# Sums of squares ahead of the two MLPs: eight stored squares added by VectorE, channel sum after the second unit

## The chip, the cores and the metric

One core of a Trainium2 chip runs the whole program. The metric is the device time of one execution in microseconds (us), lower is better. TensorE (PE) multiplies matrices, VectorE (DVE), ScalarE (ACT) and GpSimd (POOL) work element by element, SyncE (SP) issues DMAs. Each engine takes its own instructions in order and waits for the others by semaphores.

## The reference

A two-layer decoder trunk on 512 tokens of width 1024, all in float32. Cut to what matters:

```python
def rmsnorm(x, g):
    y = x * lax.rsqrt(jnp.mean(x * x, axis=-1, keepdims=True) + EPS)
    return y * g

for i in range(2):
    h = h + mixer_i(rmsnorm(h, norm_mix[i]))          # 0: dilated windows, 1: differential
    h = h + squared_relu_mlp(rmsnorm(h, norm_mlp[i]), w_ff1[i], w_ff2[i])
    h = h + sigmoid(rmsnorm(h, norm_ple[i]) @ w_ple_gate[i]) * (p[i] @ w_ple_proj[i])
out = rmsnorm(h, final_norm)
# squared_relu_mlp: a = relu(h @ w1); return (a * a) @ w2,  1024 -> 4096 -> 1024
```

## The kernel before

The hidden state h is kept with channels on the 128 partitions: eight slabs (n = 0 to 7) of 128 channels by 512 tokens. Work on TensorE is cut into units. A unit makes 128 output channels: eight chunks of three matmuls of 128x512 (high times high, low times high, high times low), so 24 matmuls into one PSUM bank. For that each weight is split in two: ScalarE rounds the 128x1024 raw tile (`w_hi`, `split_hi`, L976), VectorE subtracts (`w_lo`, `split_lo`, L1284). Activations are split alike (`act_hi` L991, `act_lo` L1299). `next_hi(u)` and `next_lo(u)` split the weights of unit u+1. There are two sets of split weights, by the parity of the unit, so the split of unit u waits until unit u-2 is done: `wait(sc, units_done, u - 1)`.

Ahead of each MLP stands `out_late`. The attention's output projection has one (layer 0) or two (layer 1) late units that come slab by slab in PSUM, and the MLP's first unit is put between: for each slab VectorE adds the projection to h (L1529, L1532), ScalarE makes `act_hi` and the square (L1001, L1004), VectorE makes `act_lo` of the slab before, and TensorE does that slab's chunk of the first unit. So chunk n of the first unit waits for `act_lo` n.

The norm: the squares of the eight slabs are summed (the first one is written to `sumsq`, the other seven pass through two buffers `square`, and GpSimd adds each, L956). One matmul with ones sums over channels into bank `attn` (`statistics` on TensorE, L1828, two passes). ScalarE takes the root (L1009, which needs another activation table), VectorE the reciprocal `rstd` (L1304). `rstd` is applied only where a unit leaves PSUM: `scaled` = bank x `rstd` (L1552), `hidden` = max(scaled, 0) x scaled (L1555), `act_hi` (L1142), `act_lo` (L1558).

The banks set how late that may be. The MLP's first unit has `unit_out1`, the second `unit_out0`, the third `misc` (`is_third`), and the fourth `unit_out0` again. Thus the fourth unit of an MLP waits until the second has been read by L1552 (`wait(te, evac_done, ...)` in `unit`), and this comes after `rstd` and after the whole of the first unit's four steps in VectorE's order.

SyncE loads the raw weights ahead (`load`, L731), each once the split of the unit two before is done.

Of the kernel before, what the change touches and what calls it, by code (L numbers as in the profile page):

```python
# [33 lines left out]
F32 = mybir.dt.float32  # L34
F32R = mybir.dt.float32r
ALU = mybir.AluOpType
ACT = mybir.ActivationFunctionType

P = 128
T = 512  # L40
# [60 lines left out]


LATE = (1, 2)


U_A = 0
# [142 lines left out]
def build(nc, x, p, rel_bias, a_w_qkv, a_w_o, b_w_qkv, b_w_o, lq1, lk1, lq2, lk2, subln, norm_mix,  # L249
          norm_mlp, w_ff1, w_ff2, norm_ple, w_gate, w_proj, final_norm, selector, out):  # L250
    ctx = ExitStack()
    with ctx:
# [26 lines left out]
        heads = sb("heads", [P, 2 * GROUPS * 3 * T])  # L279
        bias = [sb(f"bias{i}", [P, 2 * T]) for i in range(2)]  # L280
        with nc.sbuf_tensor("soft", [P, 3, B_TILES * P], F32) as soft:
            pass
        probs = [sb(f"probs{i}", [P, 2 * T]) for i in range(A_ITEMS)]
        probs_t = sb("probs_t", [P, T])
# [309 lines left out]
        x_copied = sem("x_copied")  # L594
        square_ready = sem("square_ready")
        sumsq_done = sem("sumsq_done")
        act_hi_ready = sem("act_hi_ready")
        act_ready = sem("act_ready")
        ones_ready = sem("ones_ready")
# [271 lines left out]
        def _(pool):  # L871
# [78 lines left out]
                    spread_values(step)  # L950

            for norm in range(1, 7):
                for n in range(1, KC if norm < 6 else KC - 1):
                    pool.wait_ge(square_ready, (norm - 1) * (KC - 1) + n)
                    pool.wait_ge(sumsq_done, (norm - 1) * KC + n)
                    pool.tensor_tensor(sumsq[:, :], sumsq[:, :], square[n % 2][:, :],  # L956
                                       ALU.add).then_inc(sumsq_done, 1)
                for head in range(B_HEADS) if norm == 3 else ():
                    spread_head(head)
# [3 lines left out]
        def _(sc):  # L963
# [30 lines left out]
            def slab(w, n, h, dst, written, count):  # L994

                wait(sc, written, count)
                if dst is not None:
                    slab_hi(w, n, h, dst)
                if n == 0:
                    wait(sc, stat_ps, w // KC)  # L1000
                    sc.activation(sumsq[:, :], h[:, n, :], ACT.Square).then_inc(sumsq_done, 1)  # L1001
                else:
                    wait(sc, sumsq_done, w - 1 - KC)
                    sc.activation(square[w % 2][:, :], h[:, n, :], ACT.Square  # L1004
                                  ).then_inc(square_ready, 1)
# [114 lines left out]
            def out_late(layer, first, w0, h, dst):  # L1120

                late = LATE[layer]
                if layer:
                    for i in range(late):
                        next_hi(At(first + KC + i))
                for n in range(KC):
                    if n < KC - 1:
                        slab(w0 + n, n, h, dst, late_added, layer * (KC - 1) + n + 1)
                    else:
                        slab(w0 + n, n, h, dst, evac_done, first + KC + late)  # L1130

            def mlp_of(layer, first, norm, h):
                def up(u, k, n, is_first):
                    two_ahead = u.reg is None
                    if is_first or not two_ahead:
                        next_hi(u)
                    if two_ahead and n < KC - 1:
                        next_hi(u + 1)
                    if is_first:
                        statistics(norm)  # L1140
                    wait(sc, hid_ready, k + 1)
                    sc.activation(MID[layer][0][:, n, :], hidden[:, :], ACT.Copy  # L1142
                                  ).then_inc(hid_hi_ready, 1)
                    if layer == 0 and two_ahead and n == 1:
                        split_ple_hi(0)

                def down(u, q, n, last):
                    if last:
                        add_slab(u, (norm + 1) * KC + n, n, h, IN[layer])
                    else:  # L1150
                        next_hi(u)
                mlp(sc, layer, first, up, down)
# [124 lines left out]
        def _(ve):  # L1277
# [241 lines left out]
            def out_late(layer, first, w0, h, dst):  # L1519

                late = LATE[layer]
                u = first + KC + late - 1
                if layer:
                    for i in range(late):
                        next_lo(At(first + KC + i))
                for n in range(KC):
                    if n < KC - 1:
                        ve.wait_ge(late_ps, layer * (KC - 1) + n + 1)
                        ve.tensor_tensor(h[:, n, :], h[:, n, :], wide_bank(n), ALU.add).then_inc(late_added, 1)  # L1529
                    else:  # L1530
                        ve.wait_ge(units_done, u + 1)
                        ve.tensor_tensor(h[:, n, :], h[:, n, :], wide_bank(n), ALU.add).then_inc(evac_done, late)  # L1532
                    if n:
                        slab_lo(w0 + n - 1, n - 1, h, dst)
                    if layer == 0 and n == 5:
                        ve.wait_ge(units_done, first + KC)
                        ve.tensor_tensor(h[:, KC - 1, :], h[:, KC - 1, :], misc[:, :], ALU.add
                                         ).then_inc(evac_done, 1)
                        ve.wait_ge(evac_done, first + KC)
                slab_lo(w0 + KC - 1, KC - 1, h, dst)  # L1540

            def mlp_of(layer, first, norm, h):
                def up(u, k, n, is_first):
                    two_ahead = u.reg is None
                    if is_first or not two_ahead:
                        next_lo(u)
                    if two_ahead and n < KC - 1:
                        next_lo(u + 1)
                    if is_first:
                        statistics(norm)  # L1550
                    wait(ve, units_done, u + 1)
                    ve.tensor_tensor(scaled[:, :], bank_of(u)[:, :], rstd[:, :], ALU.mult  # L1552
                                     ).then_inc(evac_done, 1)
                    wait(ve, evac_done, u + 1)
                    ve.scalar_tensor_tensor(hidden[:, :], scaled[:, :], 0.0, scaled[:, :],  # L1555
                                            ALU.max, ALU.mult).then_inc(hid_ready, 1)
                    wait(ve, hid_hi_ready, k + 1)
                    ve.tensor_tensor(MID[layer][1][:, n, :], hidden[:, :], MID[layer][0][:, n, :],  # L1558
                                     ALU.subtract).then_inc(hid_done, 1)
                    if layer == 0 and two_ahead and n == 1:  # L1560
                        split_ple_lo(0)

                def down(u, q, n, last):
# [190 lines left out]
        def _(te):  # L1754
# [274 lines left out]

            def mlp_of(layer, first, norm):  # L2030
                def up(u, k, n, is_first):
                    if is_first:
                        statistics(norm)
                    else:
                        whole(u, IN[layer])
                    if layer == 0 and u.reg is None and n == 1:
                        turn_ple(0)
# [189 lines left out]
```

## Time and profile before

| | us |
|---|---|
| median of 3 runs | 1580.41 (1580.26 to 1580.99) |
| the profiled execution, whole | 1581.12 |
| its span, first to last record | 1579.3 |
| PE busy | 1557.7 (99%) |
| DVE busy | 930.8 (59%) |
| ACT busy | 585.7 (37%) |
| POOL busy | 502.3 (32%) |
| mean granted clock of TensorE | 0.996 |

The profiled execution is 1.82 us longer than its span, and 0.71 us longer than the median. A busy PE means that a matmul is in the pipeline; consecutive matmuls of 128x512 last 0.39 us each but start every 0.227 us. Times in the rows count from the span's start. Line numbers are those of the kernel before.

### The profile page before, as it was taken

The numbers are of one execution on the slowest core, as the hardware profiler recorded it, in microseconds if no ns is written. First come the engines' busy times: TensorE is split into PE (matmuls) and PEld (weight loads), VectorE is DVE, ScalarE is ACT, GpSimd is POOL, SyncE is SP. The second block draws the span as 40 slices with busy tenths as digits, with TensorE's granted clock in tenths as the row PEclk, the third lists the DMA queues.
The fourth block names the chain that finished last, engine by engine and source line by source line (L and its number), as shares of the span: only waits on it lengthen the run. The fifth ranks groups of instructions, "written<-read, shape, count | busy, mean of one in ns | idle before, by whom it ended". The sixth has DMA issues, their size and how long they took to land.

```text
span 1579.3 us, 22036 instructions
## 1 busy us (share of the span) xinstructions
PE 1557.7 (99%) x7890; PEld 1282.6 (81%) x7890; DVE 930.8 (59%) x1569; ACT 585.7 (37%) x1056; POOL 502.3 (32%) x900
## 2 busy tenths in 40 slices
PE   9999999999999999999999999999999999999998
PEld 7788888888888788888888878888778888888887
DVE  6466466567456854536355677778585453635565
ACT  5223324314324522212223445777452221312344
POOL 4067578488491200000001126888420000000111
PEclk9999999999999999999999999999999999999998
DMA  6565566465443233333333344454333333333331
GB/s 171 141 171 154 143 166 158 143 171 144 122 132 109 79 102 93 95 102 90 99 93 93 101 122 141 123 138 130 101 93 94 94 104 96 93 95 91 100 110 71
DMA packets 327204, 184.37 MB, mean 117 GB/s; under 512 B 44857, under 2 KB 312690, under 8 KB 327138
## 3 DMA queue, kind: packets, MB, share of 16 engines
q1 hardware_dynamic: 300112, 158.61, 35.3%
q0 software_dynamic: 26768, 24.88, 6.0%
q8 instruction: 38, 0.62, 0.2%
q14 instruction: 28, 0.23, 0.1%
q10 hardware_dynamic: 258, 0.04, 0.0%
HBM read 157.11 MB, written 10.60 MB: 106 GB/s over the span
## 4 chain that ended last, share of the span: by engine, by line
PE 81%; POOL 10%; DVE 2%; DMA 2%; SPq 2%; ACT 2%; issue 1%; POOLq 0%; ACTq 0%; DVEq 0%
PE unit_out L1757 22%; PE unit_out L1759 22%; PE unit_out L1758 22%; POOL probs L919 8%; POOL sumsq L956 1%; PE attn L2117 1%; PE unit_out L1922 1%; PE attn L1905 1%; SPq L763 1%; PE unit_out L1923 1%; PE unit_out L1924 1%; DMA w_raw<-in_a_w_qkv_dram 1%; DMA probs<-blocks 1%; DVE w_lo L1284 1%; PE misc L1757 1%
## 5 line engine op out<-in xcount | busy, mean ns | idle before, releaser
L1757 PE MATMUL unit_out<-act_hi,w_hi 128*128 128x512 f32 x1849 | 724.4, 392 | 2.4 <-DVE act_lo L1299 1.2
L1759 PE MATMUL unit_out<-act_hi,w_lo 128*128 128x512 f32 x1849 | 718.2, 388 | 0.0
L1758 PE MATMUL unit_out<-act_lo,w_hi 128*128 128x512 f32 x1849 | 718.0, 388 | 0.0
L976 ACT ACTIVATE w_hi<-w_raw 128x1024 fp32r<-128x1024 f32 (+3 forms) x256 | 271.2, 1059 | 505.8 <-PE unit_out L1759 412.3
L1757 PEld LDWEIGHTS unit_out<-act_hi,w_hi 128*128 128x128 f32 x1849 | 347.2, 188 | 78.6 <-DVE w_lo L1284 4.5
L1759 PEld LDWEIGHTS unit_out<-act_hi,w_lo 128*128 128x128 f32 x1849 | 347.2, 188 | 71.9
L1758 PEld LDWEIGHTS unit_out<-act_lo,w_hi 128*128 128x128 f32 x1849 | 347.4, 188 | 69.8 <-issue 0.2
L1284 DVE TENSOR_TENSOR w_lo<-w_raw,w_hi 128x1024 fp32r<-128x1024 f32 (+3 forms) x256 | 320.2, 1251 | 114.5 <-ACT w_hi L976 114.2
L956 POOL TENSOR_TENSOR sumsq<-sumsq,square 128x512 f32<-128x512 f32 x41 | 57.9, 1411 | 843.3 <-ACT square L1004 841.6
L919 POOL DMA_DIRECT2D probs<-blocks x448 | 221.3, 503 | 135.2 <-DVE blocks L1377 109.1
L928 POOL DMA_DIRECT2D heads<-probs_t x256 | 139.1, 552 | 67.4 <-DVE probs_t L1377 67.0
L1142 ACT ACTIVATE act_hi<-hidden 128x512 fp32r<-128x512 f32 x64 | 40.5, 633 | 243.4 <-DVE hidden L1555 243.4
L1552 DVE TENSOR_TENSOR scaled<-unit_out,rstd 128x512 f32<-128x512 f32 x62 | 42.8, 690 | 67.7 <-PE unit_out L1759 67.6
L1363 DVE TENSOR_TENSOR h_a<-h_a,unit_out 128x512 f32<-128x512 f32 x39 | 26.8, 688 | 90.0 <-PE unit_out L1759 90.0
L1363 DVE TENSOR_TENSOR heads<-heads,unit_out 128x512 f32<-128x512 f32 x40 | 27.5, 687 | 86.8 <-PE unit_out L1759 86.8
L928 POOL DMA_DIRECT2D soft<-soft_blocks x128 | 76.0, 602 | 7.4 <-issue 5.4
L1085 ACT ACTIVATE probs<-probs,w_raw 128x256 f32<-128x256 f32 (+1 forms) x128 | 61.7, 483 | 28.3 <-DVE w_raw L1393 28.3
L1558 DVE TENSOR_TENSOR act_lo<-hidden,act_hi 128x512 fp32r<-128x512 f32 x64 | 44.3, 693 | 44.7 <-ACT act_hi L1142 44.7
L1555 DVE SCALAR_TENSOR_TENSOR hidden<-scaled 128x512 f32<-128x512 f32 x64 | 44.3, 692 | 2.2
L1201 ACT ACTIVATE soft<-soft,low 128x512 f32<-128x512 f32 (+3 forms) x64 | 35.1, 551 | 7.2 <-DVE low L1639 7.1
L1468 DVE TENSOR_TENSOR act_lo<-attn,act_hi 128x512 f32 (+1 forms) x8 | 5.5, 692 | 53.0 <-ACT act_hi L1095 53.0
L1372 DVE TENSOR_SCALAR probs<-probs,w_raw 128x256 f32<-128x256 f32 (+1 forms) x128 | 35.5, 342 | 0.3
(316 smaller groups left out, 1399.8 us busy)
## 6 DMA issues: line engine op xcount, KB each, us to landing
w_raw<-in_w_ff_dram SPq DMA_DIRECT2D x128, 512.0 KB, 4.0
w_raw<-in_a_w_qkv_dram SPq DMA_DIRECT2D x56, 512.0 KB, 4.4
probs<-blocks POOLq DMA_DIRECT2D x448, 32.0 KB, 2.5
w_raw<-in_b_w_qkv_dram SPq DMA_DIRECT2D x24, 512.0 KB, 4.2
w_raw<-in_a_w_qkv_dram SPq DMA_DIRECT2D x32, 256.0 KB, 3.1
w_raw<-in_w_ple_gate_dram SPq DMA_DIRECT2D x16, 512.0 KB, 4.0
soft<-soft_blocks POOLq DMA_DIRECT2D x128, 40.0 KB, 1.9
heads<-probs_t POOLq DMA_DIRECT2D x256, 16.0 KB, 2.7
```

The source lines that it names most:

```text
L919: pool.dma_start(turned_order(to[j * SUB:(j + 1) * SUB, :])[:, i, :], turned_order(blocks_of[i * SUB:(i + 1) * SUB, :])[:, j, :]).then_inc ...
L928: pool.dma_start(to[j * SUB:(j + 1) * SUB, :, i, :], of[i * SUB:(i + 1) * SUB, j, :, :]).then_inc(landed, 16)
L956: pool.tensor_tensor(sumsq[:, :], sumsq[:, :], square[n % 2][:, :], ALU.add).then_inc(sumsq_done, 1)
L976: sc.activation(weights_of(u)[0][:, 0:width, :], w_raw[par][:, 0:width, :], ACT.Copy).then_inc(hi_done, 1)
L1085: e = sc.activation(probs[ph][:, cols], probs[ph][:, cols], ACT.Exp, bias=low_col, scale=-1.0, accum_out=sum_col)
L1284: ve.tensor_tensor(lo[:, 0:width, :], w_raw[par][:, 0:width, :], hi[:, 0:width, :], ALU.subtract).then_inc(lo_done, 1)
L1363: ve.tensor_tensor(h[:, n, :], h[:, n, :], unit_out[u.const % 2][:, :], ALU.add).then_inc(evac_done, 1)
L1555: ve.scalar_tensor_tensor(hidden[:, :], scaled[:, :], 0.0, scaled[:, :], ALU.max, ALU.mult).then_inc(hid_ready, 1)
L1558: ve.tensor_tensor(MID[layer][1][:, n, :], hidden[:, :], MID[layer][0][:, n, :], ALU.subtract).then_inc(hid_done, 1)
L1757: te.matmul(bank, w_k[0], hi, start=start, stop=False)
L1758: te.matmul(bank, w_k[0], lo, start=False, stop=False)
L1759: return te.matmul(bank, w_k[1], hi, start=False, stop=stop)
```

## The change

For the norms ahead of the two MLPs (numbers 1 and 4 in `TREE_NORMS`) three things are different. ScalarE writes the eight squares to eight places of a new tile `squares`, in memory that the attention's tiles had, without waiting for anyone. GpSimd adds nothing there. VectorE adds them in three instructions (`add_squares`: 2048, 1024 and 512 elements a partition) once all eight are there. TensorE's matmul with ones stands after the second unit instead of after the first. ScalarE loads the table of the root ahead, with a root of one column.

Besides, weights are split at other places. The second unit's are split inside `out_late`, on ScalarE before slab 6 and on VectorE before the add of slab 7 (before: after all slabs). The third's and the fourth's are split before the root and the reciprocal (before: the fourth's after the first unit's `act_lo`), and each later one a unit earlier in the code.

```diff
+TREE_NORMS = (1, 4)
...
+        with nc.sbuf_tensor("squares", [P, KC, T], F32) as squares:
...
-                for n in range(1, KC if norm < 6 else KC - 1):
+                for n in range(1, KC if norm < 6 else KC - 1) if norm not in TREE_NORMS else ():
...
-                if n == 0:
+                if w // KC in TREE_NORMS:
+                    last = sc.activation(squares[:, n, :], h[:, n, :], ACT.Square)
+                    if n == KC - 1:
+                        last.then_inc(square_ready, KC - 1)
+                elif n == 0:
...
                 for n in range(KC):
+                    if n == KC - 2:
+                        next_hi(At(first + KC + late))
...
                 def up(u, k, n, is_first):
-                    two_ahead = u.reg is None
-                    if is_first or not two_ahead:
+                    ahead = u.reg is None
+                    if not ahead:
                         next_hi(u)
-                    if two_ahead and n < KC - 1:
+                    if is_first:
                         next_hi(u + 1)
-                    if is_first:
+
+                        sc.activation(spare[:, :], eps_col[:, 0:1], ACT.Sqrt)
+                        next_hi(u + 2)
                         statistics(norm)
...
+                    if ahead and 0 < n < KC - 2:
+                        next_hi(u + 2)
...
                 for n in range(KC):
+                    if n == KC - 1:
+                        next_lo(At(first + KC + late))
...
+            def add_squares(norm):
+
+                k = 2 * TREE_NORMS.index(norm)
+                ve.wait_ge(square_ready, norm * (KC - 1))
+                ve.tensor_tensor(squares[:, 0:4, :], squares[:, 0:4, :], squares[:, 4:8, :], ALU.add
+                                 ).then_inc(squares_added, 1)
+                ve.wait_ge(squares_added, k + 1)
+                ve.tensor_tensor(squares[:, 0:2, :], squares[:, 0:2, :], squares[:, 2:4, :], ALU.add
+                                 ).then_inc(squares_added, 1)
+                ve.wait_ge(squares_added, k + 2)
+                ve.wait_ge(stat_ps, norm)
+                ve.tensor_tensor(sumsq[:, :], squares[:, 0, :], squares[:, 1, :], ALU.add
+                                 ).then_inc(sumsq_done, KC)
...
-                    if is_first:
+                    if u.reg is None and n == 2:
                         statistics(norm)
-                    else:
+                    if not is_first:
                         whole(u, IN[layer])
```

VectorE in layer 0, from the add of slab 6 to the read of the second unit. Before (h_a is the hidden state, the first `scaled` belongs to the first unit, the second to the second):

```order
L1529 TENSOR_TENSOR h_a<-h_a,turned 128x512
L1299 SCALAR_TENSOR_TENSOR act_lo<-h_a,gains,act_hi 128x512
L1532 TENSOR_TENSOR h_a<-h_a,turned 128x512
L1299 SCALAR_TENSOR_TENSOR act_lo<-h_a,gains,act_hi 128x512 x2
L1284 TENSOR_TENSOR w_lo<-w_raw,w_hi 128x1024 x2
L1304 RECIPROCAL rstd<-root 128x512
L1552 TENSOR_TENSOR scaled<-unit_out,rstd 128x512
L1555 SCALAR_TENSOR_TENSOR hidden<-scaled 128x512
L1558 TENSOR_TENSOR act_lo<-hidden,act_hi 128x512
L1284 TENSOR_TENSOR w_lo<-w_raw,w_hi 128x1024
L1552 TENSOR_TENSOR scaled<-unit_out,rstd 128x512
```

And now, the same stretch of the same engine:

```order
L1313 SCALAR_TENSOR_TENSOR act_lo<-h_a,gains,act_hi 128x512
L1298 TENSOR_TENSOR w_lo<-w_raw,w_hi 128x1024
L1548 TENSOR_TENSOR h_a<-h_a,turned 128x512
L1313 SCALAR_TENSOR_TENSOR act_lo<-h_a,gains,act_hi 128x512 x2
L1562 TENSOR_TENSOR squares<-squares 128x2048
L1565 TENSOR_TENSOR squares<-squares 128x1024
L1569 TENSOR_TENSOR sumsq<-squares 128x512
L1298 TENSOR_TENSOR w_lo<-w_raw,w_hi 128x1024 x2
L1318 RECIPROCAL rstd<-root 128x512
L1583 TENSOR_TENSOR scaled<-unit_out,rstd 128x512
L1586 SCALAR_TENSOR_TENSOR hidden<-scaled 128x512
L1589 TENSOR_TENSOR act_lo<-hidden,act_hi 128x512
```

The second unit's `w_lo` has moved ahead of slab 7's add, three adds stand behind the slabs, and three units' `w_lo` instead of two stand ahead of the reciprocal.

ScalarE in layer 0, from slab 5's square on, now (before, the first `w_hi` stood with the second one, behind the last square, and the third `w_hi` behind the first `act_hi` of hidden):

```order
L1004 ACTIVATE squares<-h_a 128x512
L980 ACTIVATE w_hi<-w_raw 128x1024
L995 ACTIVATE act_hi<-h_a,gains 128x512
L1004 ACTIVATE squares<-h_a 128x512
L995 ACTIVATE act_hi<-h_a,gains 128x512
L1004 ACTIVATE squares<-h_a 128x512
L980 ACTIVATE w_hi<-w_raw 128x1024
L1150 ACT_TABLE_LOAD
L1150 ACTIVATE spare<-eps_col 128x1
L980 ACTIVATE w_hi<-w_raw 128x1024
L1017 ACTIVATE root<-attn,eps_col 128x512
```

The second unit's `w_hi` stands in front of the `act_hi` of slabs 6 and 7, and the fourth unit's in front of the root.

TensorE in layer 0, around the end of the second unit, now (the transposes of `bias` are those of the layer's p; before, the matmul on `sumsq` stood ahead of the second unit):

```order
L1792 MATMUL unit_out<-act_hi,w_lo 128x512
L1866 MATMUL logits<-ident,bias 128x128 x8
L1861 MATMUL attn<-sumsq,ones 128x512
L1790 MATMUL misc<-act_hi,w_hi 128x512
L1791 MATMUL misc<-act_lo,w_hi 128x512
```

The channel sum now follows the second unit, and in layer 0 the eight transposes too. Nothing else on TensorE moves, and its number of instructions is the same.

## Rows read from the trace of the kernel before

**Rows 1.** The page, part 1: busy us, share of the span, instructions.

```profile
PE 1557.7 (99%) x7890; PEld 1282.6 (81%) x7890; DVE 930.8 (59%) x1569; ACT 585.7 (37%) x1056; POOL 502.3 (32%) x900
```

**Rows 2.** Timeline of PE, layer 1: start, us, engine line, tiles [idle before].

```profile
1159.04 0.39 PE L1759 MATMUL turned<-act_hi,w_lo 128*128 128x512 f32 x1
...
1160.40 0.39 PE L1759 MATMUL unit_out<-act_hi,qk_hi 128*128 128x512 f32 x1
...
1164.41 0.50 PE L1757 MATMUL unit_out<-act_hi,qk_hi 128*128 128x512 f32 x1 [0.73 <-DVE act_lo L1299]
...
1165.56 1.12 PE L1828 MATMUL attn<-sumsq,ones 128*128 128x512 f32 x2 [0.18 <-POOL sumsq L956]
1166.64 0.50 PE L1757 MATMUL unit_out<-act_hi,w_hi 128*128 128x512 f32 x1
...
1172.26 0.39 PE L1757 MATMUL misc<-act_hi,w_hi 128*128 128x512 f32 x1
...
1177.70 0.39 PE L1757 MATMUL unit_out<-act_hi,w_hi 128*128 128x512 f32 x1
```

**Rows 3.** Timeline of DVE, layer 1.

```profile
1160.89 0.67 DVE L1532 TENSOR_TENSOR heads<-heads,turned 128x512 f32<-128x512 f32 x1
1161.48 2.88 DVE L1299 SCALAR_TENSOR_TENSOR act_lo<-heads,gains,act_hi 128x512 fp32r<-128x512 f32 x2
...
1168.57 3.35 DVE L1304 RECIPROCAL rstd<-root 128x512 f32<-128x512 f32 x1 [0.78 <-ACT root L1009]
1171.96 0.69 DVE L1552 TENSOR_TENSOR scaled<-unit_out,rstd 128x512 f32<-128x512 f32 x1
...
1174.07 0.69 DVE L1558 TENSOR_TENSOR act_lo<-hidden,act_hi 128x512 fp32r<-128x512 f32 x1 [0.70 <-ACT act_hi L1142]
1175.02 1.23 DVE L1284 TENSOR_TENSOR w_lo<-w_raw,w_hi 128x1024 fp32r<-128x1024 f32 x1 [0.26 <-ACT w_hi L976]
1176.16 0.68 DVE L1552 TENSOR_TENSOR scaled<-unit_out,rstd 128x512 f32<-128x512 f32 x1
```

**Rows 4.** Timeline of ACT, layer 1.

```profile
1161.59 0.72 ACT L991 ACTIVATE act_hi<-heads,gains 128x512 fp32r<-128x512 f32 x1 [0.46 <-DVE heads L1532]
...
1165.48 1.06 ACT L976 ACTIVATE w_hi<-w_raw 128x1024 fp32r<-128x1024 f32 x1 [1.69 <-PE unit_out L1759]
1166.55 1.28 ACT L1009 ACT_TABLE_LOAD   x1
1167.85 0.69 ACT L1009 ACTIVATE root<-attn,eps_col 128x512 f32<-128x512 f32 x1
```

**Rows 5.** Lines L1299 and L1284, layer 0's slabs: duration ns min/median/max.

```profile
L1299 DVE SCALAR_TENSOR_TENSOR act_lo<-h_a,gains,act_hi x7: 747/1184/1772, 521.8 to 531.3; 128x512 fp32r<-128x512 f32 x7
...
L1284 DVE TENSOR_TENSOR w_lo<-w_raw,w_hi x1: 2296/2296/2296, 533.0 to 533.0; 128x1024 fp32r<-128x1024 f32 x1
```

**Rows 6.** Timeline of PE, layer 0.

```profile
530.45 0.39 PE L1757 MATMUL unit_out<-act_hi,qk_hi 128*128 128x512 f32 x1
...
535.33 0.50 PE L1757 MATMUL unit_out<-act_hi,w_hi 128*128 128x512 f32 x1
...
540.91 1.04 PE L1833 MATMUL logits<-ident,bias 128*128 128x128 f32 x8
541.70 0.47 PE L1757 MATMUL misc<-act_hi,w_hi 128*128 128x512 f32 x1
...
547.27 0.39 PE L1757 MATMUL unit_out<-act_hi,w_hi 128*128 128x512 f32 x1
```

**Rows 7.** Timeline of PE: the same 20 matmuls at two times.

```profile
1105.90 2.47 PE L2117 MATMUL attn<-heads,soft 128*128 128x128 f32 x20 [0.15 <-issue]
...
1127.88 3.95 PE L2117 MATMUL attn<-heads,soft 128*128 128x128 f32 x20 [2.66 <-issue]
```

**Rows 8.** Windows: us, busy by engine, PEclk (granted clock), DMA share, GB/s.

```profile
1128.40:1129.00 0.60, 0.60 (x5) 0.60 (x4) 0.00 (x0) 0.00 (x0) 0.00 (x0) 0.50 0.92 276
...
1163.00:1164.00 1.00, 0.68 (x3) 0.20 (x2) 1.00 (x1) 0.79 (x1) 0.86 (x2) 1.00 0.00 0
```

More of the change, by code:

```diff
@@ L281, in build @@
         with nc.sbuf_tensor("soft", [P, 3, B_TILES * P], F32) as soft:
+            pass
+        with nc.sbuf_tensor("squares", [P, KC, T], F32) as squares:
             pass
@@ L596, in build @@
         sumsq_done = sem("sumsq_done")
+        squares_added = sem("squares_added")
         act_hi_ready = sem("act_hi_ready")
@@ L1143, in up @@
                                   ).then_inc(hid_hi_ready, 1)
-                    if layer == 0 and two_ahead and n == 1:
+                    if ahead and 0 < n < KC - 2:
+                        next_hi(u + 2)
+                    if layer == 0 and ahead and n == 1:
                         split_ple_hi(0)
@@ L1540, in out_late @@
                 slab_lo(w0 + KC - 1, KC - 1, h, dst)
+            def add_squares(norm):
[10 more added lines that the diff above has]
+                                 ).then_inc(sumsq_done, KC)
             def mlp_of(layer, first, norm, h):
                 def up(u, k, n, is_first):
-                    two_ahead = u.reg is None
-                    if is_first or not two_ahead:
+                    ahead = u.reg is None
+                    if not ahead:
                         next_lo(u)
-                    if two_ahead and n < KC - 1:
+                    if is_first:
+                        add_squares(norm)
                         next_lo(u + 1)
-                    if is_first:
+                        next_lo(u + 2)
                         statistics(norm)
@@ L1559, in up @@
                                      ALU.subtract).then_inc(hid_done, 1)
-                    if layer == 0 and two_ahead and n == 1:
+                    if ahead and 0 < n < KC - 2:
+                        next_lo(u + 2)
+                    if layer == 0 and ahead and n == 1:
                         split_ple_lo(0)
@@ L2031, in up @@
                 def up(u, k, n, is_first):
-                    if is_first:
+                    if u.reg is None and n == 2:
                         statistics(norm)
-                    else:
+                    if not is_first:
                         whole(u, IN[layer])
```

## The prediction

> **What bounds the kernel now.** I read the page's busy times first: TensorE is busy 99% of the span [rows 1], so a change off TensorE counts only where TensorE stands still. Next came TensorE's timeline around the two places that the change touches, the start of each MLP. A unit of 24 matmuls takes 5.44 us there (1172.26 to 1177.70 [rows 2]), 0.227 us a matmul, and the only stops are the last chunks of the first unit and the channel sum. In layer 1 chunk 5 could have started at 1160.62, 0.22 after the last matmul of chunk 4 began at 1160.40 [rows 2]. Three chunks of 0.68 later the second unit could have started at 1162.66. It started at 1166.64: 3.98 us, of which the channel sum is 1.08 (1165.56 to 1166.64) and 2.9 are stops. In layer 0 the same stretch runs from 530.45 to 535.33 [rows 6], which is 4.88, or 2.84 above 2.04: 1.76 of stops. So at most 4.66 us can be had from both places.
>
> The stops come from VectorE's `act_lo`. One takes 0.747 us at its shortest, 1.184 in the median and 1.772 at its longest, and a `w_lo` of 1.23 us [rows 3] took 2.296 in the midst of them [rows 5]; both read two tiles of SBUF while GpSimd adds squares. The adds from PSUM stay at 0.67 to 0.69 [rows 3]. By the Trainium skill (SBUF — State Buffer, "SBUF: two separate sides") the port pair that both engines share is held for a whole instruction and the loser fully blocks. The trace agrees, with the 2.296 against 1.23; if it did not hold, the late `act_lo` would keep their 1.18, and the result would be the upper bound below.
>
> **The second unit's split, ahead of slabs 6 and 7 (a new wait).** I work in layer 1's times. ScalarE's `w_hi` needs the late unit done, whose last matmul ends at 1159.04 + 0.39 = 1159.43 [rows 2]. With 0.10 for the semaphore it runs 1159.53 to 1160.59 (1.06 [rows 4]). VectorE waits for it in front of slab 7's add: `w_lo` 1160.63 to 1161.86 (1.23), the add from 1161.78 to 1162.45 (0.67; back to back the next starts some 0.08 before the end of one), `act_lo` 6 from 1162.38 to 1163.13 (0.75). TensorE's chunk 6 starts at 1163.19, though it could have at 1161.30: a stop of 1.9. Slab 7's `act_hi` (0.72 [rows 4]) ends at 1163.21 and its `act_lo` at 1164.00; chunk 7 starts at 1164.06 instead of 1164.41 [rows 2], the second unit 0.80 later, at 1164.86 instead of 1166.64. That is 1.78 earlier: the channel sum is gone from there (1.08), and 0.7 of stops. Layer 0 is the same stretch 630.17 earlier (530.45 against 1160.62), so its second unit starts at 534.69 instead of 535.33, 0.64 earlier.
>
> **The adds.** Seven GpSimd adds leave each place. VectorE's three are not in the trace. A `w_lo` of 1024 elements takes 1.23 and an add of 512 takes 0.67 to 0.69 [rows 3], so 1.05 ns an element: 2.3 + 1.23 + 0.69, with waits 4.3 us. They start when the last square is there, 1164.0, and end at 1168.3. The second unit hides them: it ends at 1170.48 (5.62 long, 1166.64 to 1172.26). The cost is nothing, up to 2.2 us more of it too. A price as slow as the longest `act_lo`, 1.772 for 512, would bring 12.4 us and cost 10 per place; nothing on GpSimd disturbs them, so I take 4.3. By the Trainium skill (GPSIMD Engine Reference, "Engine selection") an elementwise add belongs on VectorE, GpSimd being about 2 times slower with two inputs. By that rule alone the move is a gain; it leaves out who queues behind the adds on VectorE.
>
> **The channel sum.** It costs 1.08 behind the second unit as before it. The third unit starts at 1170.48 + 1.08 = 1171.56 instead of 1172.26, 0.7 earlier, and would be done at 1177.00. In layer 0 the second unit is done at 534.69 + 5.58 = 540.27 (535.33 to 540.91), the transposes take 0.79 to 541.06 (540.91 to 541.70 [rows 6]), the sum 1.08: third unit at 542.14 instead of 541.70, done 5.57 later at 547.71.
>
> **The root and the reciprocal, late now.** The table load (1.28 [rows 4]) is hidden, but the fourth unit's `w_hi` stands ahead of the root and needs the second unit done: 1170.64 + 0.10 to 1171.80. The root takes 0.69, to 1172.50, while VectorE makes that `w_lo` to 1173.07. The reciprocal of 3.35 [rows 3] starts at about 1173.0 and ends at 1176.35. Before, it ended at 1171.92. So `rstd` is 4.4 us later. From there the first unit's four steps take 2.84 (1171.92 to the end of `act_lo`, 1174.07 + 0.69 = 1174.76 [rows 3]). Before, a `w_lo` (1175.02, 1.23) stood between that and the second unit's read at 1176.16, which now comes at once: 1179.15 to 1179.84. This saves 1.45. TensorE's fourth unit needs this read, since it writes the same bank: it starts at 1179.9 instead of 1177.70. Before, the read was over at 1176.84, 0.86 us ahead of need; now TensorE stands from 1177.00 to 1179.9. **Layer 1: +2.2 us.** In layer 0 the sum's end at 542.25 gates the root: root to 542.95, reciprocal to 546.33, second unit read by 549.85, fourth unit at 549.9 instead of 547.27 [rows 6]. **Layer 0: +2.6 us.** Behind the `act_lo` of the second unit only one `w_lo` (in layer 0 also p's) precedes the third unit's read: 555.2 in layer 0, just under the 555.3 at which the fifth unit wants it. From there each unit has 5.44 us for less than 4.2 of VectorE's work, so nothing more is lost and nothing is given back.
>
> Sum without a fall of the clock: +4.8 us.
>
> **The clock.** Between 1125.2 and 1127.88 TensorE stood still for 2.66 us; then the granted clock was 0.50, which is 1.2 GHz [rows 8], and 20 matmuls took 3.95 instead of 2.47 [rows 7]: 1.5 us. Three stops of up to 0.73 in a row left it at 1.00, 2.4 GHz [rows 2, 8]. The new stops lie between: 1.7 to 1.9 at chunk 6 in each layer, 2.0 to 2.2 ahead of layer 0's fourth unit, 2.7 to 2.9 ahead of layer 1's. The last is as long as the one that made it fall, so I count one fall, +1.5; the others may add 1.5 each, or none fall.
>
> Forecast: 1581.12 + 4.8 + 1.5 = 1587.4 for the profiled execution, which stood 0.71 above the median; from the median, 1580.41 + 6.3 = **1586.7 us**. Without a fall 1585.2, with three 1589.7, with four 1591.2. If `act_lo` kept 1.18 us, chunk 7 and all that hangs on it would be 0.86 later per layer: 1588.4. Each of the two sums of steps may be off by 0.5.
>
> **Rivals.** (a) No change: `rstd` is in time. It would need the fourth unit's `w_hi` not to hold the root, or the bank to be free otherwise. Without the new wait at the fourth unit, the third unit's shifts are what is left, -0.7 and +0.4: 1580.1. For it speaks that before there were 0.86 us of room; against it, that `rstd` moves by 4.4 and only 1.45 is saved behind it. (b) Faster, the other side: the GpSimd port conflict was what held TensorE, and neither the early split nor the late root takes its place. Then all stops go, 1.76 + 2.9 = 4.66: 1575.8. It decides this way if the second unit's `w_lo` is done before slab 6's `act_hi` is wanted and the second unit's bank is read by 1177.0 in layer 1. The late unit ends at 1159.43, though, and two splitting steps of 2.3 us in a row follow it. (c) Three or more falls of the clock: 1589.7 to 1591.2, the mechanism of the forecast at a higher price.
>
> **Chances.** The forecast with none to two falls 0.76, (c) 0.10, (a) 0.10, (b) 0.04. The forecast's own range is 1584.7 to 1588.7. The range that should hold the time 8 times in 10 goes from 1583.3, where half of a stop is missing, to 1589.9, with three falls. About 0.2% (3.2 us) is what a measurement can tell from no change, so the line is at 1583.6: slower 0.85, within 0.11, faster 0.04.
>
> **What would show it.** TensorE idle ahead of the fourth unit of each MLP, 2 and 2.8 us, ended by VectorE's read of the second unit's bank; none before. A stop of some 1.8 us ahead of chunk 6 and hardly any ahead of chunk 7. `act_lo` of 0.75 us throughout. Reciprocals that start 5.7 (layer 0) and 4.4 us later. The three adds done over 2 us before the channel sum. A granted clock of 0.5 for some us after a stop, in layer 1 first. Wrong I would be if the fourth units start without a stop, or if ScalarE makes the root before the fourth unit's `w_hi`.

## The result, and the profile after

The changed kernel takes 1588.36 us in the median of 6 runs (1586.66 to 1593.61), the kernel before 1580.70 in 6 runs on the same chip: a ratio of 1.0052, 95% interval 1.0041 to 1.0062. A second set, beside 29 runs of before, gave 1586.27 against 1579.21, 1.0050 (1.0037 to 1.0063). It is slower, by 7 to 8 us; 6.3 were forecast (1586.7). The profiled execution of the changed kernel took 1586.66, the one of before 1581.12.

The page of the changed kernel, part 1, answers to [rows 1]:

```profile
PE 1558.0 (98%) x7890; PEld 1283.1 (81%) x7890; DVE 931.0 (59%) x1575; ACT 586.2 (37%) x1058; POOL 480.2 (30%) x886
```

TensorE does the same work in the same busy time. GpSimd lost 22 us and 14 instructions, and the time did not fall with them. What grew is TensorE's idle time. Its two largest waits (what for, us in total, times, longest):

```profile
PE unit_out L1790 <- DVE scaled L1583: 5.1, 2, 2.9
PE unit_out L1790 <- DVE act_lo L1313: 4.5, 5, 1.7
```

The first line is new: it is the fourth unit of each MLP, which waits for VectorE to read the second unit's bank. TensorE's timeline in layer 1, to be read beside [rows 2]:

```profile
1161.33 0.39 PE L1792 MATMUL turned<-act_hi,w_lo 128*128 128x512 f32 x1
...
1165.45 0.50 PE L1790 MATMUL unit_out<-act_hi,qk_hi 128*128 128x512 f32 x1 [1.69 <-DVE act_lo L1313]
...
1172.59 1.02 PE L1861 MATMUL attn<-sumsq,ones 128*128 128x512 f32 x2
1173.05 0.80 PE L1790 MATMUL misc<-act_hi,w_hi 128*128 128x512 f32 x1
...
1182.02 0.66 PE L1790 MATMUL unit_out<-act_hi,w_hi 128*128 128x512 f32 x1 [2.92 <-DVE scaled L1583]
1182.48 0.63 PE L1791 MATMUL unit_out<-act_lo,w_hi 128*128 128x512 f32 x1
1182.91 0.63 PE L1792 MATMUL unit_out<-act_hi,w_lo 128*128 128x512 f32 x1
```

Two stops, at chunk 6 and at the fourth unit. Behind the second one matmuls take 0.63 instead of 0.39, and the granted clock is 0.50 (the third number from the right):

```profile
1183.00:1184.00 1.00, 1.00 (x4) 0.81 (x3) 0.69 (x1) 1.00 (x2) 0.00 (x0) 0.50 0.00 0
```

Layer 0, beside [rows 6], has the same two stops, without a slower clock behind them:

```profile
527.68 0.39 PE L1792 MATMUL turned<-act_hi,w_lo 128*128 128x512 f32 x1
...
531.80 0.50 PE L1790 MATMUL unit_out<-act_hi,qk_hi 128*128 128x512 f32 x1 [1.69 <-DVE act_lo L1313]
...
548.53 0.47 PE L1790 MATMUL unit_out<-act_hi,w_hi 128*128 128x512 f32 x1 [2.22 <-DVE scaled L1583]
```

VectorE in layer 1, beside [rows 3]. `act_lo` is down to 0.75 a piece (1.63 for two, with a gap of 0.13 between them), the tree takes 4.3, and the reciprocal stands behind everything:

```profile
1162.91 1.23 DVE L1298 TENSOR_TENSOR w_lo<-w_raw,w_hi 128x1024 fp32r<-128x1024 f32 x1 [1.43 <-ACT w_hi L980]
...
1164.65 1.63 DVE L1313 SCALAR_TENSOR_TENSOR act_lo<-heads,gains,act_hi 128x512 fp32r<-128x512 f32 x2
1166.19 2.29 DVE L1562 TENSOR_TENSOR squares<-squares 128x2048 f32<-128x2048 f32 x1
1168.51 1.23 DVE L1565 TENSOR_TENSOR squares<-squares 128x1024 f32<-128x1024 f32 x1
1169.83 0.69 DVE L1569 TENSOR_TENSOR sumsq<-squares 128x512 f32<-128x512 f32 x1
...
1173.94 1.23 DVE L1298 TENSOR_TENSOR w_lo<-w_raw,w_hi 128x1024 fp32r<-128x1024 f32 x1 [2.28 <-ACT w_hi L980]
1175.08 3.35 DVE L1318 RECIPROCAL rstd<-root 128x512 f32<-128x512 f32 x1
...
1181.19 0.68 DVE L1583 TENSOR_TENSOR scaled<-unit_out,rstd 128x512 f32<-128x512 f32 x1
```

The read ends at 1181.87 and the fourth unit starts at 1182.02. And ScalarE, beside [rows 4]: the root does come behind the fourth unit's `w_hi`.

```profile
1172.85 1.06 ACT L980 ACTIVATE w_hi<-w_raw 128x1024 fp32r<-128x1024 f32 x1 [2.88 <-PE unit_out L1792]
1173.81 0.67 ACT L1017 ACTIVATE root<-attn,eps_col 128x512 f32<-128x512 f32 x1
```

**One yardstick for all kernels.** Whole executions of one kernel scatter by some us, so I read each profile at the two places alone. Zero is the start of the late unit's last matmul: 1159.04 in layer 1 of before [rows 2], and in layer 0 of before this one:

```profile
528.86 0.39 PE L1759 MATMUL turned<-act_hi,w_lo 128*128 128x512 f32 x1
```

The table has the starts of the second, fourth and eighth unit behind that zero; the eighth minus that of before is what the place cost. "Both places" is the sum of that over the two layers, from one profiled execution of each kernel. The last column is the difference between the median of all executions and that of the kernel before, run beside them. The names are explained under the experiments.

| kernel | layer 0: 2nd, 4th, 8th | layer 1: 2nd, 4th, 8th | both places | medians |
|---|---|---|---|---|
| before | 6.47, 18.41, 40.17 | 7.60, 18.66, 40.42 | 0 | 0 |
| changed | 5.80, 20.85, 42.73 | 5.80, 20.69, 44.15 | +6.3 | +7.7 |
| changed, again | 5.80, 20.86, 44.37 | 5.79, 20.67, 43.99 | +7.8 | +7.1 |
| few columns | 4.66, 16.64, 38.40 | 4.73, 15.74, 37.50 | -4.7 | -5.0 |
| tree only | 8.09, 21.39, 43.15 | 8.17, 20.33, 42.09 | +4.7 | +5.0 |
| late split | 4.66, 19.87, 41.75 | 4.72, 19.72, 43.21 | +4.4 | +5.0 |
| filler | 5.79, 20.87, 42.75 | 5.82, 20.72, 42.59 | +4.8 | +5.8 |
| free bank | 5.80, 18.49, 40.83 | 5.81, 17.60, 40.67 | +0.9 | +2.9 |
| root first | 5.81, 21.99, 43.88 | 5.81, 21.11, 44.46 | +7.8 | +10.0 |
| bank, late split | 4.66, 17.46, 39.81 | 4.72, 16.63, 39.72 | -1.1 | -0.6 |
| + fifth's split | 4.66, 17.50, 40.04 | 4.73, 16.65, 38.46 | -2.1 | -1.9 |
| + square last | 4.14, 16.98, 39.53 | 4.20, 16.16, 37.98 | -3.1 | -3.6 |

### The profile page after: what moved, and what is told of

Same layout as the page of the kernel before. It is cut to its first block, busy times and chain, and to the rows that moved or that the text cites. A ratio compares the mean times of both kernels' runs of the same rounds, so it can differ in the third digit from the quotient of the medians.

```text
span 1584.9 us, 22018 instructions
## 1 busy us (share of the span) xinstructions
PE 1558.0 (98%) x7890; PEld 1283.1 (81%) x7890; DVE 931.0 (59%) x1575; ACT 586.2 (37%) x1058; POOL 480.2 (30%) x886
## 4 chain that ended last, share of the span: by engine, by line
PE 85%; POOL 6%; DVE 3%; DMA 2%; ACT 2%; SPq 2%; issue 1%; ACTq 0%; DVEq 0%
PE unit_out L1790 24%; PE unit_out L1792 23%; PE unit_out L1791 23%; POOL probs L923 6%; PE attn L2150 1%; PE attn L1938 1%; PE unit_out L1955 1%; PE unit_out L1956 1%; PE unit_out L1957 1%; SPq L767 1%; DMA w_raw<-in_a_w_qkv_dram 1%; DVE w_lo L1298 1%; ACT w_hi L980 1%; DVE rstd L1318 1%; PE logits L1917 1%
## 5 line engine op out<-in xcount | busy, mean ns | idle before, releaser
L960 POOL TENSOR_TENSOR sumsq<-sumsq,square 128x512 f32<-128x512 f32 x27 | 35.9, 1331 | 871.8 <-ACT square L1012 871.8
```

## The experiments

The edits are shown shortened. In brackets stands the name in the table, and how many executions the median is of.

**What GpSimd's adds cost by themselves (few columns, 9).** The kernel before; the other columns of two norms' sums are left out.

```
-  pool.tensor_tensor(sumsq[:, :], sumsq[:, :], square[n % 2][:, :], ...)
+  few = slice(0, 8 if norm in (1, 4) else T)
+  pool.tensor_tensor(sumsq[:, few], sumsq[:, few], square[n % 2][:, few], ...)
```

> The kernel before, in which GpSimd adds only 8 of the 512 columns of each square at the two norms ahead of the MLPs (the other columns of these norms' sums are left out); order and waits are untouched. It asks what GpSimd's long adds cost TensorE by themselves. If they are the whole reason for the stops in the first unit's last chunks (VectorE's act_lo of 1.18 and w_lo of 2.30 shrink to 0.75 and 1.23), the second units start 4.7 us behind the last late matmul instead of 6.47 (layer 0) and 7.60 (layer 1), the channel sum still ahead of them: 4.7 less than before, about 1574.5 to 1575.5 against 1579.2. If the stops come from the chain from slab to slab on ScalarE and VectorE anyway, act_lo gets shorter and the second units start at most 1 us earlier each: 1577.5 or more.

Measured: 1574.25 against 1579.26, 0.9968 (0.9956 to 0.9980). VectorE around layer 1's slabs:

```profile
1160.97 1.63 DVE L1300 SCALAR_TENSOR_TENSOR act_lo<-heads,gains,act_hi 128x512 fp32r<-128x512 f32 x2
1163.32 1.22 DVE L1285 TENSOR_TENSOR w_lo<-w_raw,w_hi 128x1024 fp32r<-128x1024 f32 x1 [0.72 <-ACT w_hi L977]
```

Two `act_lo` take 1.63 where they took 2.88 [rows 3], and the second units start at 4.66 and 4.73, the channel sum still ahead of them. TensorE has no stop left at either place. So GpSimd's long adds, which slowed `act_lo` and `w_lo`, were the whole reason for the stops in the first units, and 5 us were there to be had. What the change put in their place ate these 5 us, and 7 to 8 more. The runs show that VectorE is slow beside these adds; that it is a port which the two share is not shown by them.

**The tree alone (tree only, 5).** The kernel before, with the squares in eight places and VectorE's tree at the head of the MLP; no split and no sum is moved.

```
+  if is_first:
+      add_squares(norm)
```

> The kernel before with one part of the change alone: the squares kept in eight places and added by VectorE (ahead of the second unit's `w_lo`), no GpSimd, but the channel sum still in front of the second unit and all splits where they were. Main theory: `act_lo` takes 0.75 us and the last chunks run without stops, but TensorE then stands about 3.3 us until the adds are done; the second unit starts 0.5 (layer 1) and 1.6 us (layer 0) later than in the kernel before, and the clock may fall in each stop (1.5 each): 1582.9 without, 1585.9 with two falls. Rival (the port conflict with GpSimd is what costs in the kernel before, and the adds are cheap on VectorE): 1577 to 1579.

Measured: 1584.32 against 1579.28, 1.0035 (1.0022 to 1.0048). TensorE in layer 0 and layer 1:

```profile
535.30 1.94 PE L1852 MATMUL attn<-sumsq,ones 128*128 128x512 f32 x2 [3.17 <-DVE sumsq L1561]
...
1167.42 2.07 PE L1852 MATMUL attn<-sumsq,ones 128*128 128x512 f32 x2 [3.21 <-DVE sumsq L1561]
```

The second units start 0.57 (layer 1) and 1.62 us (layer 0) later than before; 0.5 and 1.6 were expected, and the time lies between the 1582.9 without a fall of the clock and the 1585.9 with two. Most of the tree shows where nothing hides it: TensorE stands for 3.2 of its 4.3 us. The two matmuls of the sum take 1.94 and 2.07 instead of 1.12, at a granted clock that falls to 0.50 there in both layers. Moving the sum behind the second unit was needed to hide the tree, but it was not enough: with all its parts the change costs more (+7.1 to +7.7) than the tree left in the open (+5.0). In the changed kernel it is hidden: `sumsq` is there at 1170.52, the sum is wanted at 1172.59.

**The fourth unit on a free bank (free bank, 11).** The changed kernel; the bank is `turned`, idle there.

```
-  return misc if is_third(u) else unit_out[u.const % 2]
+  return misc if is_third(u) else turned[:, 0:T] if is_fourth(u) else unit_out[u.const % 2]
-  wait(te, evac_done, u - (3 if is_first_up(u) else 2 if is_third(u) else 1))
+  wait(te, evac_done, u - frees(u))   # 3 for the fourth to the sixth unit as well
```

> The changed kernel, but the fourth unit of each MLP writes to a free bank (the first half of `turned`), so that it need not wait until VectorE has read the second unit; the fifth and sixth units wait only for the bank that they really reuse. Main theory (the late `rstd` holds the fourth unit through its bank): the stops of 2.2 and 2.9 us ahead of the fourth units are gone and with them the fall of the clock; the next thing late is the fifth unit's `w_lo`, worth a stop of up to 1 us. The fifth unit then starts 0.5 (layer 0) and 0.1 us (layer 1) later than in the kernel before, so about 1581.3 against 1580.7 of before, some 7 us less than the changed kernel. Rival (it is VectorE's 4.3 us of adds, or the early split of the second unit, that costs): the time stays above 1585, the stop only moves to the fifth unit in full.

Measured: 1582.21 against 1579.28, 1.0017 (1.0008 to 1.0026). The stops ahead of the fourth units are gone, and what is late next are the fifth units, on `w_lo`:

```profile
555.13 0.50 PE L1802 MATMUL unit_out<-act_hi,w_hi 128*128 128x512 f32 x1 [0.28 <-DVE w_lo L1310]
...
1186.29 0.50 PE L1802 MATMUL unit_out<-act_hi,w_hi 128*128 128x512 f32 x1 [0.99 <-DVE w_lo L1310]
```

Both places now cost 0.9 instead of 6.3, so 5.4 us hung on the bank. The 0.28 and 0.99 are the same lateness one step on, since the fifth unit's `w_lo` stands on VectorE behind the late reads of the banks; without them the places would stand at -0.4. The median says 2.9, with an interval of 1.3 to 4.1 us that leaves out the 0.9; more on that below.

**Root and reciprocal first (root first, 5).** The changed kernel, on ScalarE and on VectorE:

```
-  next_hi(u + 2)
   statistics(norm)
+  next_hi(u + 2)
```

> The changed kernel with the root ahead of the fourth unit's w_hi on ScalarE and the reciprocal ahead of its w_lo on VectorE. Theory (the fourth unit waits for the sum of VectorE's work behind the channel sum, and for no one piece of it: 3.35 reciprocal, 2.84 for the first unit, 0.69 for the second, and the w_lo of 1.23 wherever it stands behind the sum): in layer 0 the w_lo, which ran in idle time ahead of the reciprocal (540.28 to 541.50), now stands behind it, so that the fourth unit starts 1.15 later; in layer 1 the root starts only 0.15 earlier, since the channel sum ends at about 1173.6, the reciprocal 0.7 earlier, and the w_lo behind it takes 1.15: 0.4 later. Both stops are then over 3.3 us long and the clock falls behind both: 1.6 us slower than the changed kernel with two falls, 1587.5 to 1589 where that one has 1586.3 and before 1579.2. Rival (what holds the fourth unit is that the fourth unit's split stands ahead of the root): rstd is there up to 1.2 us earlier in layer 1 and the stops shrink to 2.2 or less; 1585 or less.

Measured: 1589.28 against 1579.26, 1.0058 (1.0043 to 1.0074). VectorE in layer 0, then TensorE at both fourth units:

```profile
543.51 3.35 DVE L1318 RECIPROCAL rstd<-root 128x512 f32<-128x512 f32 x1 [3.60 <-ACT root L1017]
546.90 1.22 DVE L1298 TENSOR_TENSOR w_lo<-w_raw,w_hi 128x1024 fp32r<-128x1024 f32 x1
548.04 0.68 DVE L1583 TENSOR_TENSOR scaled<-unit_out,rstd 128x512 f32<-128x512 f32 x1
```

```profile
551.58 0.47 PE L1790 MATMUL unit_out<-act_hi,w_hi 128*128 128x512 f32 x1 [3.35 <-DVE scaled L1583]
...
1184.87 0.76 PE L1790 MATMUL unit_out<-act_hi,w_hi 128*128 128x512 f32 x1 [3.35 <-DVE scaled L1583]
```

The fourth units start 1.14 and 0.42 later than in the changed kernel (table: 21.99 against 20.85, 21.11 against 20.69); 1.15 and 0.4 were expected. That the fourth unit's split stands ahead of the root was thus no cause: VectorE's work behind the channel sum is a sum of pieces, and the change's order hid one of them in layer 0 and a part of it in layer 1. One thing came out otherwise: the clock was expected to fall behind both stops, and in this execution it fell in layer 1 alone.

**The second unit's split behind the last slab (late split, 6).** The changed kernel:

```
-  if n == KC - 2: next_hi(At(first + KC + late))     # in ScalarE's loop over the slabs
-  if n == KC - 1: next_lo(At(first + KC + late))     # in VectorE's
+  next_hi(At(first + KC + late))                     # behind the loops
+  next_lo(At(first + KC + late))
```

> The changed kernel, but the second unit's weights are split behind slab 7 on ScalarE and VectorE, as in the kernel before, and not ahead of slabs 6 and 7. Main theory: chunks 6 and 7 of the first unit run without a stop (1.7 us before chunk 6 now), a stop of about 1.1 us ahead of the second unit takes its place, the second unit starts 1.1 us earlier in each layer, and the stops ahead of the fourth units stay at 2.2 and 2.9: 2.2 us less than the changed kernel, 1586.2. Rival (the early split is the whole loss): 1580 to 1582. Rival (the early split is hidden, as the late `rstd` decides alone): no change, 1588.4.

Measured: 1584.25 against 1579.28, 1.0034 (1.0022 to 1.0046). TensorE, layer 1:

```profile
1164.89 0.50 PE L1788 MATMUL unit_out<-act_hi,w_hi 128*128 128x512 f32 x1 [0.90 <-DVE w_lo L1297]
...
1179.89 0.47 PE L1788 MATMUL unit_out<-act_hi,w_hi 128*128 128x512 f32 x1 [2.92 <-DVE scaled L1581]
```

The stop of 1.69 at chunk 6 becomes one of 0.87 and 0.90 ahead of the second unit, which starts 1.1 earlier in each layer. The stop ahead of the fourth unit keeps its 2.92: everything behind the second unit's end, the root too, hangs on that end. So the main theory held, and the early split is neither the whole loss nor hidden.

**The idle time filled (filler, 5).** The changed kernel, with 20 transposes of the identity between the third and fourth unit.

```
+  if u.reg is None and n == 3:
+      for _ in range(20):
+          te.transpose(turned[:, 0:P], ident[:, :], ident[:, :])
```

> The changed kernel, with 20 transposes of the identity into a free bank between the third and the fourth unit of each MLP, about 2 us of work that fits into the stop. Main theory (part of the loss is the clock that falls in the longer stop): the granted clock stays at 1.00 through the start of the fourth unit in layer 1 and its first eight matmuls take 0.39 instead of 0.63 us, the fourth units start no later, and the time is 1.6 us less for each fall avoided: 1586 to 1587 in the median. Rival (the clock falls for another reason, or the transposes are not hidden): the same time or up to 4 us more.

Measured: 1585.11 against 1579.28, 1.0038 (1.0025 to 1.0051). TensorE, layer 1:

```profile
1177.80 2.34 PE L2069 MATMUL turned<-ident 128*128 128x128 f32 x20
...
1180.87 0.47 PE L1790 MATMUL unit_out<-act_hi,w_hi 128*128 128x512 f32 x1 [0.73 <-DVE scaled L1583]
```

The fourth units start when they did (20.87 and 20.72), the granted clock stays at 1.00, and the eighth unit in layer 1 stands at 42.59 instead of 44.15. So of layer 1's 3.7 us the fall of the clock was 1.6, and 2.17 are the waits.

**The changed kernel once more (again, 5).**

> The changed kernel once more, unchanged. Around the two MLP starts its profile showed 6.3 us more than before (stops, and one fall of the clock), but the medians differed by 7.7. If this second profile shows the same 6.3 around the two places while the rest of the run is as long as before, what is left over is scatter between runs, and the difference of the medians should come out at 6 to 7 us. If there is a third place where the changed kernel loses time, the difference stays at 7.5 or more, and this profile, should it come from a run near the median, shows a stretch outside the two places that is over 1 us longer than in the other profiles.

Measured: 1586.27 against 1579.21. The profiled execution has the same stops, but in layer 0 too the clock falls. TensorE, then the windows (us, busy by engine, granted clock, DMA share, GB/s) around that unit:

```profile
548.34 0.47 PE L1790 MATMUL unit_out<-act_hi,w_hi 128*128 128x512 f32 x1 [2.21 <-DVE scaled L1583]
...
550.05 0.63 PE L1790 MATMUL unit_out<-act_hi,w_hi 128*128 128x512 f32 x1
```

```profile
549.00:551.00 2.00, 2.00 (x8) 1.53 (x7) 1.13 (x2) 2.00 (x3) 0.00 (x0) 0.63 0.00 0
551.00:552.50 1.50, 1.50 (x5) 1.21 (x4) 1.50 (x2) 0.44 (x1) 0.00 (x0) 0.50 0.00 0
```

Neither of my two expectations was right. The places do not always cost 6.3: they cost 6.3 or 7.8, as the clock falls once or twice. A third place where the changed kernel loses time does not show: from layer 0's eighth unit to layer 1's zero its two executions take 590.92 and 588.77 us, that of before 590.01, and behind the second place 379.4 and 379.5 against 379.8. The medians, 7.1 and 7.7, lie between the two costs.

**Towards a better version (11, 11 and 12).** First, free bank and late split together:

> The changed kernel with both edits of the first two experiments: the fourth unit of each MLP writes a bank that nobody reads at that time, and the second unit's split stands behind the first unit's last slab. Theory (the two stops are independent, each costs what it showed): against the free bank alone, both MLP starts gain what the late split gained by itself, 1.0 us each, so that the fifth units start 1.1 us (layer 0) and 1.3 us (layer 1) after those of before minus 2.0 in sum: 0.4 less minus 1.5, that is about 1.1 to 1.5 us less than before; 1577.8 to 1578.4 against 1579.3. The stops ahead of the fifth units (0.28 and 0.99 on w_lo) grow by at most the 1.0 that TensorE is earlier. Rival (VectorE's chain of splits and reads is the bound there, whatever TensorE does ahead of it): the fifth units start when they did with the free bank alone, the stops on w_lo grow to 1.2 and 2.0, and the time stays at 0.9 above before.

Measured: 1578.60 against 1579.21, 0.9996 (0.9987 to 1.0005). At the two places -1.1, and 2.0 less than with the free bank alone, as the theory had it; the median gains 0.6 of the expected 0.9 to 1.5, and its interval (-2.1 to +0.8 us) does not tell it from no change. The stops ahead of the fifth units stayed (0.29 and 0.99). Then the fifth unit's split one step earlier, in both engines' `up`:

```
+  if ahead and n == 0: next_hi(u + 3)      # next_lo(u + 3) on VectorE
-  if ahead and 0 < n < KC - 2:
+  if ahead and 1 < n < KC - 2:
       next_hi(u + 2)
```

> The experiment with free bank and late split, and w_hi and w_lo of the fifth unit made one step earlier, behind the first unit's act_lo instead of behind the second unit's. Theory (w_lo of the fifth unit is the last stop of the late root and reciprocal): the stops on w_lo ahead of the fifth units go, since that w_lo ends some 4 us earlier, and no read comes too late for it; each MLP start gains the length of its stop. About 2.5 to 3.5 us less than before: 1576 to 1577 against 1579.3. Rival (the read of the second unit, now behind that w_lo, takes its place as the stop): the fifth units start as late as they did, ended by VectorE's read, and the time is that of the experiment without the move.

Measured: 1577.32 against 1579.21, 0.9989 (0.9980 to 0.9998). Layer 1's stop went whole (the eighth unit 1.26 earlier). In layer 0 it came back one unit later, 0.48 on the sixth's `w_lo`, which stands behind the split of `p` (`ple_lo`, 1.23, at 554.32 on VectorE). So 1.9 us less than before (2.1 at the places), where 2.5 to 3.5 were expected. Last, the square of slab 7 behind the second unit's `w_hi`:

```
   slab_hi(w, n, h, dst)
+  if between is not None:
+      next_hi(between)
   last = sc.activation(squares[:, n, :], h[:, n, :], ACT.Square)
```

> As the one with the fifth unit's split moved, and the last square of the first unit behind the second unit's w_hi on ScalarE instead of ahead of it. Theory (ahead of the second unit TensorE waits for ScalarE's 0.6 us square and then the split of 1.06 and 1.23): the stop of 0.9 ahead of the second unit shrinks to 0.3 in each layer; VectorE's tree of adds starts 1.06 - 0.6 = 0.5 later or so and is still hidden behind the second unit. 1.1 us less than without this edit. Rival (VectorE is not waiting for ScalarE there): no difference.

Measured: 1575.66 against 1579.21, 0.9980 (0.9972 to 0.9989). TensorE at layer 1's second unit:

```profile
1158.98 0.50 PE L1805 MATMUL unit_out<-act_hi,w_hi 128*128 128x512 f32 x1 [0.40 <-DVE w_lo L1312]
```

0.93 became 0.40, and the second units start 0.52 and 0.53 earlier; the two places gain 1.0 of the expected 1.1. That is the best version: 3.6 us below before (interval 1.7 to 4.4) and 10.6 below the changed kernel on the same chip, with the same tree and the same place of the channel sum.

## Why the prediction was right

Its own steps, each time measured from the last late matmul:

- **Chunk 6.** A stop of 1.9 was worked out, as a delay of the start. The chunk starts 1.85 after it could have; the profile's 1.69 counts from the end of the matmul before. The second unit starts 0.67 and 1.80 earlier (0.64 and 1.78 predicted). The late split removed this stop, put 0.87 and 0.90 in its place, and left the one ahead of the fourth unit as it was.
- **The conflict with GpSimd.** `act_lo` at 0.75 throughout: 744 to 753 ns. The 4.66 us that the prediction put on all stops is what the few-columns kernel gained, 4.7. So rival (b) had the cause of the old stops right, and failed where it said that no new wait takes their place.
- **The tree.** 4.3 us predicted, 4.33 measured (1166.19 to 1170.52), hidden by the second unit. Shown by the tree-only kernel, where it isn't.
- **The channel sum.** Put at 1.08 in either place, with 5.62 for the unit in front of it and 5.44 for the one behind, 12.14 in all. In layer 1 of the free-bank kernel the two units and the sum take 11.79 (5.81 to 17.60): the term is too large by 0.35. It is of little weight, since the fourth unit waits for VectorE anyway.
- **Root and reciprocal.** The reciprocal was put 13.96 (1173.0) and 14.09 (542.95) behind the zero and started at 13.75 and 13.91, that is 4.2 and 5.5 later than before (4.4 and 5.7 predicted). The reasons held too: in layer 1 the root ended at 1174.48 and the `w_lo` that the reciprocal stands behind at 1175.17, in layer 0 the root waited for the channel sum. The fourth units were put at 20.86 (1179.9) and 21.04 (549.9) and started at 20.69 and 20.85: +2.0 and +2.4 for +2.2 and +2.6. The free bank, which removed both stops, shows that it is through the bank that the late `rstd` holds TensorE.
- **Nothing more behind it.** The fifth unit follows at 5.56 in layer 0 (26.41), all later ones at 5.44. Right, but for 0.1.
- **The clock.** One fall of 1.5 was counted, with "the others may add". It is 1.4 to 1.6 a fall at the fourth units, in layer 1 always (three executions with the 2.92 stop), in layer 0 in one of three (with 2.2). So the mean is nearer to 1.3 falls than to 1, which is some 0.5 of the 0.8 to 1.4 us that the forecast of 6.3 lacked; the medians' intervals (6.5 to 9.8 us and 5.8 to 9.9 us) leave open what the rest is.

That the forecast's 6.3 and the first profile's +6.3 agree to a tenth is partly luck: that execution had one fall, the next one two. For the price of 10 us per place that the prediction gives to slow adds it shows no working, and no run had slow adds.

Rival (a) failed as it said: without the wait at the bank the places cost +0.9, and with the wait they cost +6.3. It put the third unit's shifts at -0.7 and +0.4; they are -1.06 and +0.08 (17.60 against 18.66, 18.49 against 18.41), by the 0.35 of the channel sum. Its other condition, a root that the fourth unit's `w_hi` does not hold, was no way out: with the root first the stops grew to 3.35. Rival (c) had three falls or more; two are the most that a profile shows at the two places, and chunk 6's 1.69 left the clock at 1.00 in each.

**What stays open.** Single executions of one kernel differ by up to 7 us. The profiles show two places for this that no edit touches. One is the first unit that waits for weights, at about 50 us. That stop was 0.83 before, 1.54 with bank and late split, and 0.42 in the best version's profile, 2.01 with the root first and 2.70 with the free bank, and over 3 us in two others, here the slowest execution of the few-columns kernel:

```profile
52.69 0.50 PE L1758 MATMUL unit_out<-act_hi,w_hi 128*128 128x512 f32 x1 [3.14 <-DVE w_lo L1285]
```

In the four executions with a stop of 2.01 or more there, the granted clock then fell to 0.50; in the eight with 1.54 or less it stayed at 1.00. The zero of layer 0 lies at 529.59 to 531.44 in the four and at 526.60 to 528.86 in the eight. The other place is the stop of 2.6 us at about 1130 [rows 7]. The clock fell behind it in nine executions, that of before among them, and stayed in three (again, tree only, square last). Between the two places the nine took 590.0 to 590.9 us and the three 588.7 to 588.9.

So a single profile's total says little here, and the yardstick at the two places more. But the free bank's median stands 2.0 above its yardstick and root first's 2.3, where the others are within 1.4. The mean granted clock of all their executions gives a hint. In the 60 executions of before, those with a mean clock of 0.998 take 1578.1 us on average, those with 0.997 1579.5 and those with 0.996 1580.6, so some 1.3 us go with 0.001. Root first has 0.9944 in the mean of its five, against 0.9956 for the changed kernel again: 1.6 us by this estimate, a fall more, so that its profile with one fall at the two places was probably not the usual one. The free bank has 0.9964 against 0.9969 for before beside it, which makes 0.7 of its 2.0. The rest has no cause that I can show.

## What to carry to other kernels

Taking an engine out of a conflict pays only what the conflict cost (4.7 us here), so work out first what its work will queue behind on the new engine, and follow the chain to the next buffer that someone else needs: `rstd` late by 4.2 and 5.5 us did little harm by itself, but it kept a PSUM bank. When a result comes later, give the units that run on meanwhile their own banks, then order the splits by the time at which TensorE wants them. A split placed early can cost more than a late one, when it makes the work behind it wait: 1.69 at chunk 6 against 0.9 ahead of the second unit.

## What the runs showed of the hardware

- The length of the last stop alone does not tell whether the clock falls. In layer 0 a stop of 2.22 left the granted clock at 1.00, one of 2.21 in the same kernel was followed by 0.50, and one of 3.35 (root first) left it at 1.00 again, while the same 3.35 in layer 1 of that execution was followed by the fall. The windows behind the latter two, and the granted clock is again the third number from the right (at 1.00 it is 2.4 GHz, at 0.50 1.2 GHz):

```profile
551.60:554.00 2.40, 2.40 (x11) 1.96 (x12) 1.45 (x3) 1.80 (x3) 0.00 (x0) 1.00 0.05 14
1184.00:1186.00 2.00, 1.13 (x3) 0.97 (x4) 1.42 (x3) 0.52 (x1) 0.00 (x0) 0.65 0.48 146
```

  At the fourth units a fall cost 1.4 to 1.6 us. The shortest stop at these places or at 50 us that was followed by one is 2.01, and none up to 1.69 was. So I price a stop of over 2 us at its length and a chance of 1.5.
- VectorE's adds of the tree took 0.69 us for 512 elements a partition, 1.23 for 1024 and 2.29 for 2048, with no GpSimd adds beside them: some 1.04 ns an element and some 0.16 us for each instruction.
- The price of the channel sum's two matmuls depends on where they stand. Behind the second unit the next matmul starts 0.46 us after them (1172.59, 1173.05) and the two units around them take 0.9 us more than twice 5.44 (free bank). Ahead of the second unit it started 1.08 after them [rows 2], and 1.03 and 1.08 with few columns, where TensorE had no stop ahead of them. What makes the difference no run shows.
